# Expert lists of at most 64 slots multiplied in float32 from the loaded weights, in an order that alternates long and short lists

## The reference

```python
scores = sigmoid(t @ router_w)                 # 256 tokens, 16 experts
# best group of 4 experts, then the top 2 inside it
gate = one_hot(top_idx) * (top_s / sum(top_s))
out = 0
for e in range(16):
    hid = silu(t @ w1[e]) * (t @ w3[e])        # 1024 -> 512
    out = out + gate[:, e:e+1] * (hid @ w2[e]) # 512 -> 1024
```

## Time and profile before

| | us |
|---|---|
| device time, median of 3 runs | 1677.86 |
| lowest and highest run | 1669.85, 1683.95 |
| span of the profiled execution | 1680.8 |

### The profile page before, as it was taken

The page is one execution under the profiler, slowest core; times in us unless marked ns, Lnnn a source line. Parts: engine busy times, 40 slices in busy tenths (PEclk is TensorE's granted clock), DMA queues, the critical chain, the costliest instruction groups (busy, mean ns, idle before and its releaser), DMA issues.

```text
span 1680.8 us, 22984 instructions
## 1 busy us (share of the span) xinstructions
PE 1534.0 (91%) x9338; PEld 1237.4 (74%) x9338; DVE 1024.7 (61%) x1296; ACT 765.7 (46%) x923; POOL 245.0 (15%) x303
## 2 busy tenths in 40 slices
PE   3999989797669688999999979999999999999997
PEld 2778866575559667765547867789999777899996
DVE  3657446647556666777885885565445645655545
ACT  4324324452332442667675434635443646443444
POOL 0013370230232203130001450010000000000000
PEclk8999999887679888999999989989999999999999
DMA  9867610010332625799998524324455443345541
GB/s 348 291 218 274 175 39 1 7 24 7 89 99 101 240 100 200 263 340 356 340 383 308 186 100 171 138 101 172 174 188 200 151 159 142 138 151 200 185 172 69
DMA packets 152529, 294.14 MB, mean 175 GB/s; under 512 B 33534, under 2 KB 36741, under 8 KB 152424
## 3 DMA queue, kind: packets, MB, share of 16 engines
q1 hardware_dynamic: 136024, 270.50, 45.4%
q0 software_dynamic: 6464, 18.63, 3.4%
q10 hardware_dynamic: 9936, 3.54, 0.8%
HBM read 283.16 MB, written 9.49 MB: 174 GB/s over the span
## 4 chain that ended last, share of the span: by engine, by line
PE 77%; DVE 8%; issue 5%; ACT 5%; DVEq 2%; DMA 1%; POOL 1%; ACTq 1%; POOLq 0%; SPq 0%
PE psum L215 21%; PE psum L216 20%; PE psum L217 20%; PE psum L2570 2%; PE psum L3586 1%; PE psum L3610 1%; ACT w_high L180 1%; PE psum L795 1%; PE psum L1760 1%; DMA raw<-in_w_out_dram 1%; PE psum L1584 1%; DVE w_low L203 1%; DVE w_low L2460 1%; PE psum L812 1%; DVE outer L1217 1%
## 5 line engine op out<-in xcount | busy, mean ns | idle before, releaser
L185 DVE TENSOR_TENSOR w_low<-raw,w_high 128x4096 fp32r<-128x4096 f32 (+1 forms) x60 | 265.7, 4429 | 240.8 <-ACT w_high L180 240.4
L180 ACT ACTIVATE w_high<-raw 128x4096 fp32r<-128x4096 f32 (+1 forms) x62 | 223.6, 3610 | 132.5 <-DMA raw<-in_w_up_dram 87.1
L2460 DVE TENSOR_TENSOR w_low<-raw,w_high 128x2048 fp32r<-128x2048 f32 x90 | 204.5, 2300 | 44.7 <-ACT w_high L2452 44.5
L2452 ACT ACTIVATE w_high<-raw 128x2048 fp32r<-128x2048 f32 x90 | 167.7, 1906 | 4.7 <-DMA raw<-in_moe_w_dram 4.4
L217 PE MATMUL psum<-actA_high,w_low 128*128 128x256 f32 x512 | 145.1, 283 | 0.0
L216 PE MATMUL psum<-actA_low,w_high 128*128 128x256 f32 x512 | 145.1, 283 | 0.0
L215 PE MATMUL psum<-actA_high,w_high 128*128 128x256 f32 x512 | 145.1, 283 | 0.0
L215 PE MATMUL psum<-w_high,act_high 128*128 128x512 f32 x320 | 128.8, 403 | 14.8 <-DVE act_low L435 7.9
L216 PE MATMUL psum<-w_low,act_high 128*128 128x512 f32 x320 | 126.6, 396 | 0.0
L217 PE MATMUL psum<-w_high,act_low 128*128 128x512 f32 x320 | 126.5, 395 | 0.0
L215 PE MATMUL psum<-w_high,ff_high 128*128 128x512 f32 x256 | 100.1, 391 | 0.0
(11 more groups left out here) (570 smaller groups left out, 3384.6 us busy)
## 6 DMA issues: line engine op xcount, KB each, us to landing
raw<-in_moe_w_dram SPq DMA_DIRECT2D x90, 1024.0 KB, 7.1
raw<-in_w_in_dram SPq DMA_DIRECT2D x20, 2048.0 KB, 8.0
raw<-in_w_up_dram SPq DMA_DIRECT2D x16, 2048.0 KB, 8.0
raw<-in_w_down_dram SPq DMA_DIRECT2D x16, 2048.0 KB, 7.6
modw<-in_mod_w_dram SPq DMA_DIRECT2D x12, 2048.0 KB, 12.1
raw<-in_w_out_dram SPq DMA_DIRECT2D x6, 2048.0 KB, 9.0
raw<-in_w_gate_dram SPq DMA_DIRECT2D x4, 2048.0 KB, 8.4
raw<-in_moe_w_dram SPq DMA_DIRECT2D x3, 2048.0 KB, 8.1
```

The costliest lines, as they stand in the source:

```text
L180: act.activation(WH[n % NSLOT][:, 0:elems], RAW[n % NSLOT][:, 0:elems], ACT.Copy).then_inc(s_wh, 1)
L185: dve.tensor_tensor(WL[n % NSLOT][:, 0:elems], RAW[n % NSLOT][:, 0:elems], WH[n % NSLOT][:, 0:elems].bitcast(F32), ALU.subtract).then_inc( ...
L2452: act.activation(WH[n % NSLOT][:, ps], RAW[n % NSLOT][:, ps], ACT.Copy).then_inc(s_wh if h else X["fwh"], 1)
L2460: dve.tensor_tensor(WL[n % NSLOT][:, ps], RAW[n % NSLOT][:, ps], WH[n % NSLOT][:, ps].bitcast(F32), ALU.subtract).then_inc(s_wl if h else ...
```

## The change

Lists of at most 64 slots (ranks 7 to 14, eight of the twelve) are no longer split. TensorE multiplies them in float32 straight from `RAW`, with the gathered tokens (now kept in float32, `gsmall`) as the stationary operand of 64 columns. `both_halves` sends the left half of the weight columns to output partitions 0 to 63 and the right half to 64 to 127: 16 matmuls of 256 columns for a w1 or w3 panel, 8 of 512 columns for a w2 panel. Their panels need no ACT and no DVE pass; TensorE waits for the load itself (`half_loaded`). The hidden rows are turned by two 128 x 128 transposes and copied once by DVE. Result rows are written out as two halves.

The ranks of steps 1 to 12 are now 3, 9, 4, 11, 5, 14, 6, 10, 12, 13, 7, 8: long and short lists alternate up to step 8, then five short lists follow each other (steps 8 to 12), then the dense steps as before. The gathers are grouped anew (`GROUPS`): four groups of one long list and three groups of short ones, still seven gathers of 32 matmuls. POOL writes the counters that the second block's tables are made from between the stores of steps 11 and 12 (`const2_iota`), makes the attention masks ahead of the bands, and the wait for both moves from the head of the second block to their first use.

```diff
+    PLACES = (15, 3, 9, 4, 11, 5, 14, 6, 10, 12, 13, 7, 8, 2, 1, 0)
+    LISTED = [i for i in range(E) if 3 <= PLACES[i] < E - 1]
...
-    GROUPS = ((1,), (2,), (3,), (4, 5), (6, 7), (8, 9), (10, 11, 12))
+    GROUPS = ((1,), (2, 4, 6), (3,), (5,), (7,), (8, 9, 10), (11, 12))
+    GATHERED_AT = {1: 2, 3: 3, 5: 4, 6: 5, 8: 6}
+    LIST_MADE_AT = {1: 3, 2: 4, 4: 5, 6: 6}
...
+    def small(i):
+        return listed(i) and slots_of(i) <= HD
...
+    for i in LISTED:
+        if small(i):
+            unsplit.update((n_w1(i), n_w3(i), n_w2(i)))
...
     def high_half(act, n, h):
+        if n in unsplit:
+            return
...
     def low_half(dve, n, h):
+        if n in unsplit:
+            return
...
     def half_here(pe, n, h):
-        if n < H0 or h == 1:
-            pe.wait_ge(s_wl, n + 1)
+        if n in unsplit:
+            half_loaded(pe, n, h)
...
+    def both_halves(pe, bank, x, w, n, start, stop):
+        for g in range(2):
+            ins = pe.matmul(psum[HD * g:HD * (g + 1), bank, 0:n], x, w[:, n * g:n * (g + 1)], start=start, stop=stop)
+        return ins
...
     def inner_tensor(pe, i, n, bank, after=None):
+            if small(i):
+                x = gsmall[small_buffer(group_of(i))][:, k, window_of(i):window_of(i) + HD]
+                ins = both_halves(pe, bank, x, raw[:, k, :], PW // 2, k == 0, k == KT - 1)
+            for t in range(0 if small(i) else tiles_of(i)):
...
     def outer_tensor(pe, i):
+            if small(i):
+                ins = both_halves(pe, 4, hidF[:, k, :], raw[:, k, :], PW, k == 0, k == 3)
...
     def hidden_vector(dve, i):
+        if small(i):
+            dve.wait_ge(X["hT"], since("hT", turned(i) + 1))
+            dve.tensor_copy(hidF[:, :, :].rearrange("p (g c) s -> p g c s", g=2),
+                            psum[:, 2, 0:PW // 2].rearrange("p (c g s) -> p g c s", c=2, g=2)).then_inc(M["hL2"], 1)
+            return
...
     def lists_pool(pool):
+            if i == LAST:
+                const2_iota(pool)
...
     def layer_tensor(pe):
-        pe.wait_ge(C["done"], 1)
...
+            if d == 0:
+                pe.wait_ge(C["done"], 1)
```

More of the change, by code:

```diff
@@ L162, in two_block_kernel, with splits @@
     s_unit = sem("win_unit_then_list_made")
+    unsplit = set()
+    def splits(n):
+        return n - sum(1 for x in unsplit if x < n)
     s_uev = sem("win_evac")
@@ L200, in low_part @@
         if i == 0:
-            dve.wait_ge(s_wh, n + 1)
+            dve.wait_ge(s_wh, splits(n) + 1)
         ps = part(i, of, elems)
@@ L2301, in const2_pool @@
                            ).then_inc(C["pos_in"], 16)
+    def const2_pool(pool):
         pool.wait_ge(C["vec"], 1)
+        for g in range(3):
+            for t, k in ((0, slice(0, P)), (1, slice(P, 3 * P))):
+                m = cmask[:, g, k]
+                n = P * (t + 1)
+                pool.affine_select(out=m, in_=m, compare_op=ALU.is_ge, fill=NEG, base=P * t,
+                                   pattern=[[-1, n]], channel_multiplier=1)
+                pool.drain()
+                pool.affine_select(out=m, in_=m, compare_op=ALU.is_ge, fill=NEG,
+                                   base=STEPS_BACK * DIL[g] - P * t, pattern=[[1, n]], channel_multiplier=-1)
+                pool.drain()
+        pool.wait_ge(s_wdone, n_w3(LAST) + 1)
         for g, w in enumerate(WINS):
@@ L2423, in row_of @@
     def row_of(i):
-        return sum(slots_of(x) for x in range(1, i))
+        return sum(slots_of(x) for x in LISTED if x < i)
     def tiles_of(i):
@@ L2572, in gather_tensor, with gather_small_tensor, later_gather_tensor, small_buffer @@
             ins.then_inc(X["gat"], 1)
-    def gathered(g, b):
-        return gact[g % 2][:, 2 * b:2 * b + 2, :, :].rearrange("p k w n -> p (k w) n")[:, :, 0:columns_of(g)]
+    def gather_small_tensor(pe, g):
+        pe.wait_ge(X["G"], since("G", g + 1))
+        for b in range(2):
+            for x in range(4):
+                k = 4 * b + x
+                for t in range(NT):
+                    for w, ht in enumerate((htH, htL)):
+                        ins = pe.matmul(psum[:, gather_banks(g)[b], P * x:P * (x + 1)], ht[:, t, P * k:P * (k + 1)],
+                                        pickd[g % 2][:, t, :], start=(t, w) == (0, 0), stop=(t, w) == (NT - 1, 1))
+            ins.then_inc(X["gat"], 1)
+    def later_gather_tensor(pe, g, i):
+        pe.wait_ge(X["acc"], since("acc", i))
+        if small_group(g):
+            gather_small_tensor(pe, g)
+        else:
+            gather_tensor(pe, g, 0, 4)
+    def gathered(g, b):
+        if small_group(g):
+            return gsmall[small_buffer(g)][:, 4 * b:4 * b + 4, 0:columns_of(g)]
+        return gact[:, 2 * b:2 * b + 2, :, :].rearrange("p k w n -> p (k w) n")[:, :, 0:columns_of(g)]
+    def small_buffer(g):
+        return sum(1 for x in range(g) if small_group(x)) % 2
     def gather_out(g, b):
@@ L2640, in turn_hidden @@
         pe.wait_ge(M["hid"], n)
-        for c in range(4):
-            m = rows_in(i)
+        for c in range(2 if small(i) else 4):
+            m = P if small(i) else rows_in(i)
             ins = pe.transpose(psum[:, 2 + t, P * c:P * c + m], hidt[0:m, t, P * c:P * (c + 1)], ident[0:m, 0:m])
@@ L2650, in turned @@
     def turned(i):
-        return NT * i - (max(0, min(i, NLIST + 1) - 1))
+        return sum(tiles_of(x) for x in range(i))
     def outer_tensor(pe, i):
```

194 lines of the change are left out of this document (107 added, 87 removed).

## The result

The changed kernel takes 1671.6 us (median of 20 runs) where the kernel before takes 1678.3 us; the ratio is 0.9948 with an interval of 0.9929 to 0.9967, a gain of 0.5% or some 9 us where 20 were forecast.

The account below looks back on a forecast made before the run. TensorE set the pace, with loads close behind and becoming the bound after the change. Lists end 24.0 us earlier, less 4 us for the clock, leaving 20 us: 1660.8 us profiled, 1658 us median, range 1646 to 1677 us.

Parts of the forecast that it names:

- that stretch and the tail keep their length and start earlier: Behind the lists: the stretch from 903.7 to 980.6 us and the tail stay as long as before.
- so the queue should stay full: Expert loads: a long panel's half needs about 12 us, three panels of transfer 16.4 us, so slots come free in time.
- The sign that I had set for this: In steps 2 to 7, a DMA share below 0.95 would mean slots come free too late.
- The rival of a queue that isn't full: Loads around long panels: slots free late, 359 GB/s, 1671 us; upper part of the main case, no chance of its own.
- The end of the lists: Lists end at 879.6 us instead of 903.66, 24.0 us less, before the clock is counted.
- The clock's price there: First dense panel behind the short lists: 4 us lost to one low stretch over about 8 us of work.
- the matmuls: Short-list panels on TensorE: at most 3.86 us each, where a panel took 5.65 us.
- the two halves side by side: Short-panel matmuls on both output halves overlap; the rival, halves one behind the other, gives 1727 us, chance 0.04.
- the loads as the bound in the last five lists: Steps 8 to 12: DMA needs 16.4 us a list plus a store, TensorE only 12.0 us.
- POOL's counters at no cost: Counters moved ahead of the last store: even 10 us there cost nothing, since rows are first used 62 us later.
- The rival of the low clock in the short lists: Short lists at 1.2 GHz: panels up to 7.7 us, gain only 2 us, 1676 us; chance 0.26.
- SP did go on waiting for matmuls of the short lists: Steps 8 to 12: the forecast said SP no longer waits for matmuls of the lists.

Follow-up runs that it names:

- the order turned: Changed kernel with ACT splitting the next w1's first half before the row copy, and the next w3's before the SiLU: ratio 0.9856 to the kernel before.
- the kernel before with the delay: Kernel before plus two DVE additions of 128x1024 (2.5 us) ahead of the second block: ratio 1.0042 to the kernel before.

## Why the prediction was wrong

*The step that failed* is the one on what lies behind the lists: "that stretch and the tail keep their length and start earlier". The dense stretch does (76.9 us in both), the second block doesn't: 682.4 instead of 675.5 us. I had priced the clock only where TensorE gets new waits, in the lists, and had taken a block that the change doesn't touch as rigid. In its attention TensorE rests 0.95 us, and the clock falls there or not by the moment at which the block starts, which a gain in the lists moves. With the block at its lower length the changed kernel has ratios of 0.989 to 0.991 (1660 to 1663 us), near the forecast of 1658 and inside its range. That the range held the measured median of 1671.6 us as well is luck: its upper part was meant for a low clock in the short lists, which didn't come.

*The second step*: "so the queue should stay full". My reckoning had transfer, splits and matmuls of a half, but not what stands between them in ACT's order. The matmuls of a long w3 had covered the copy of rows; a short one leaves 1.73 us bare ahead of each long w1 and 1.2 us ahead of each long w3. So a pair took 35.5 us instead of 34.7, and w1(13) came late: the split of its first half began at 864.2 us where I had its landing at 860.0. Three pairs make 2.4 of these 4.2 us; the rest is not taken apart. The sign that I had set for this, a DMA share below 0.95 in steps 2 to 7, didn't show it: the share was 1.01 between 700 and 766 us, but at 374 GB/s where 384 were reckoned and 389 came with the order turned. The rival of a queue that isn't full named 1671 us, which is the measured median by luck: it has a gain of 7 us in the lists, where the second block started 17.0 us earlier and 7.0 were lost behind.

*The end of the lists*, forecast 879.6 before the clock, came at 886.77: 4.4 us from the late w1(13), 1.3 from its low clock, 1.65 from a wait for the split of w3(13) that the sum had not, less 0.2 for a faster w2. The clock's price there was 1.3 us, not 4.

*Right were* the matmuls (3.67 and 3.65 us a panel where 3.86 was the bound), the two halves side by side, the loads as the bound in the last five lists (16.2 us a list, forecast 16.4, DMA share 1.04), and POOL's counters at no cost (the dense stretch is 76.9 us in both). Of the 17.0 us, 2.2 lie ahead of the lists (w1 of step 1 starts at 656.03 instead of 658.22 us) and aren't the change's: the kernel before with the delay starts it at 653.56 us.

*The rival of the low clock in the short lists* is refuted: TensorE is busy 29.70 of 40.00 us there, and the clock is 1.00 throughout; its rests are at most 1.4 us and each stands between panels of work. This agrees with the Trainium skill, "TensorE: Matmul & The Clock Gate", section "HAM oscillation — how this bites in real kernels", where the loop that loses the clock each time waits longer than it works. SP did go on waiting for matmuls of the short lists (65.3 us), which I had excluded; with three slots and full transfers that wait is no sign of a bound.

Open stays why the rest of 0.95 us lets the clock fall in one place and a rest of 1.4 us in the lists doesn't, and where exactly the edges lie between the moments that fall and those that don't.

## What to carry to other kernels

Before a faster stage is priced, walk each helper engine's order around it: what had covered the copy or the split that stands ahead of the next one? Where a trace shows short rests of TensorE in a later stage, give that stage two lengths in the range, one for each clock, and measure a small gain at two or three artificial delays before believing or dropping it. Read a gain between two marks inside one trace, behind the last stage that has two lengths, and not from absolute starts. Fill such rests, or turn the helper's order, rather than hope for the moment.

## What was not expected of the hardware

A delay of 0.7 us made the kernel about 6 us faster by the ratios, and one of 2.5 us made the second block of the kernel before 7.1 us longer: the same 70 matmuls with the same rest of 0.94 to 0.95 us ran in 13.5 us at 2.4 GHz or in 20.5 us at 1.2 GHz. The Trainium skill, "TensorE: Matmul & The Clock Gate", section "What's actually happening", says that the hardware's look at TensorE's activity runs free of the kernel's start; the table above agrees. The same section names an idle stretch as what lets the clock fall. Here TensorE worked for 4.32 of the 5.00 us ahead of the fall in the profile of after, and in the first layer fillers in a rest of 0.95 us removed it, so on that point the measurement differs and decides.

```profile
1399.30:1404.30 5.00, 4.32 (x23) 3.15 (x23) 3.08 (x17) 4.79 (x13) 0.00 (x0) 1.00 0.62 205
```
